# A new order for side work in a two-layer encoder kernel: modulation slots, the last norms of attention, and squares

## The reference

```python
mod = silu(c) @ w_ada[l] + b_ada[l]              # 6 vectors of 1024 per sequence: shift, scale, gate, twice
h = rms_norm(x, g_attn) * (1 + scale_a) + shift_a
q_a, k_a, v_a, c_q, c_kv, k_r = split(h @ w_in)  # group A: 8 heads, 2 kv heads; group B: latent attention, 8 heads
o_a = attention(rope(rms(q_a)), rope(rms(k_a)), v_a)
o_b = attention(q from rms(c_q) @ w_uq, k and v from rms(c_kv) @ w_ukv)
x = x + gate_a * (concat(rms_norm(o_a), rms_norm(o_b)) @ w_o)
h = rms_norm(x, g_ffn) * (1 + scale_f) + shift_f
u = depthwise_conv_3(h @ w_up)                   # 2 x 2816 channels
x = x + gate_f * ((silu(gate) * val) @ w_down)
```

## Time and profile before

| | |
|---|---|
| median of 3 runs | 1179.14 us (1178.0 to 1182.05) |
| profiled execution | 1182.05 us, span 1180.1 us |
| TensorE busy | 1147.2 us, 97% |
| VectorE busy | 747.7 us, 63% |
| GpSimd busy | 580.4 us, 49% |
| ScalarE busy | 507.9 us, 43% |
| DMA | 151.68 MB, mean 129 GB/s |

### The profile page before, as it was taken

The page is one execution under the profiler, slowest core; times in us unless marked ns, Lnnn a source line. Parts: engine busy times, 40 slices in busy tenths (PEclk is TensorE's granted clock), DMA queues, the critical chain, the costliest instruction groups (busy, mean ns, idle before and its releaser), DMA issues.

```text
span 1180.1 us, 18741 instructions
## 1 busy us (share of the span) xinstructions
PE 1147.2 (97%) x6264; PEld 955.4 (81%) x6264; DVE 747.7 (63%) x1466; ACT 507.9 (43%) x922; POOL 580.4 (49%) x783
## 2 busy tenths in 40 slices
PE   9999999999999999998999999999999999999996
PEld 6897677898888887787898966799888888888886
DVE  5888666767767777688666687746774133312445
ACT  5345764354422344133444567535443134423442
POOL 2482342645555355536766324244555445454462
PEclk9999999999999999998999999999999999999998
DMA  9843620424455444554433221022433222332222
GB/s 347 322 159 122 220 73 19 161 72 161 160 174 201 165 143 173 196 179 160 149 119 108 72 72 37 19 72 82 145 131 108 96 85 95 99 107 89 89 89 72
DMA packets 44123, 151.68 MB, mean 129 GB/s; under 512 B 5138, under 2 KB 7954, under 8 KB 44052
## 3 DMA queue, kind: packets, MB, share of 16 engines
q1 hardware_dynamic: 44052, 150.77, 36.8%
HBM read 148.65 MB, written 2.10 MB: 128 GB/s over the span
## 4 chain that ended last, share of the span: by engine, by line
PE 35%; issue 31%; POOL 21%; POOLq 11%; DVE 1%; DVEq 0%; ACT 0%; ACTq 0%
POOL w_lo L600 21%; PE ps L687 11%; PE ps L688 11%; PE ps L693 11%; POOLq L602 7%; POOLq L660 2%; POOLq L658 1%; PE ps L819 1%; PE ps L808 1%; PE ps L788 0%; DVE ada_prod L1716 0%; PE ps L796 0%; DVE x L1655 0%; POOLq L613 0%; DVE h_lo L1759 0%
## 5 line engine op out<-in xcount | busy, mean ns | idle before, releaser
L600 POOL TENSOR_TENSOR w_lo<-w_raw,w_hi 128x256 fp32r<-128x256 f32 x712 | 540.4, 789 | 478.0 <-ACT w_hi L1243 445.6
L687 PE MATMUL ps<-h_hi,w_hi 128*128 128x512 f32 (+1 forms) x864 | 318.0, 368 | 5.7 <-POOLq L603 5.6
L688 PE MATMUL ps<-h_lo,w_hi 128*128 128x512 f32 (+1 forms) x864 | 317.1, 367 | 0.0
L693 PE MATMUL ps<-h_hi,w_lo 128*128 128x512 f32 (+1 forms) x864 | 316.7, 367 | 0.0
L1243 ACT CAST w_hi<-w_raw 128x1024 fp32r<-128x1024 f32 x178 | 183.4, 1048 | 197.4 <-PE ps L687 196.8
L2006 DVE SCALAR_TENSOR_TENSOR u_sb<-ps,par,u_sb 128x510 f32<-128x510 f32 x176 | 131.8, 749 | 110.5 <-ACT u_sb L1448 96.5
L687 PEld LDWEIGHTS ps<-h_hi,w_hi 128*128 128x128 f32 x864 | 163.8, 190 | 33.2 <-POOLq L603 6.8
L693 PEld LDWEIGHTS ps<-h_hi,w_lo 128*128 128x128 f32 x864 | 163.9, 190 | 26.7
L688 PEld LDWEIGHTS ps<-h_lo,w_hi 128*128 128x128 f32 x864 | 163.9, 190 | 26.0
L687 PE MATMUL ps<-a_hi,w_hi 128*128 128x512 f32 (+1 forms) x400 | 147.0, 367 | 4.1 <-DVEq L1703 4.1
L693 PE MATMUL ps<-a_hi,w_lo 128*128 128x512 f32 (+1 forms) x400 | 146.2, 365 | 0.0
(11 more groups left out here) (181 smaller groups left out, 1496.1 us busy)
## 6 DMA issues: line engine op xcount, KB each, us to landing
w_raw<-w_slots SPq DMA_DIRECT2D x178, 512.0 KB, 3.5
ada_raw<-ada_slots SPq DMA_DIRECT2D x88, 512.0 KB, 4.0
shift<-shift_slots SPq DMA_DIRECT2D x8, 512.0 KB, 12.8
x_tok<-x_rows SPq DMA_DIRECT2D x4, 512.0 KB, 9.9
x<-x_t SPq DMA_DIRECT2D x4, 512.0 KB, 13.8
y_t<-x SPq DMA_DIRECT2D x3, 512.0 KB, 2.9
y_t<-x SPq DMA_DIRECT2D x1, 256.0 KB, 2.9
y_t<-x SPq DMA_DIRECT2D x2, 128.0 KB, 2.7
```

Of the source, the lines that this page charges most:

```text
L600: nc.gpsimd.tensor_tensor(w_lo[:, j, c], w_raw[:, j, c], w_hi[:, j, c].bitcast(F32), ALU.subtract)
L687: hh = mm(out, stat[0], mov[0], start=first, stop=False)
L688: hl = mm(out, stat[0], mov[1], start=False, stop=False)
L693: return mm(out, stat[1], mov[0], start=False, stop=last)
```

## The change

It moves work within the queues and removes or adds none.

- In the plan, group 0's up-projection has 11 takes of modulation slots where it had 8, group 1's 12 where it had 11; the last down tile (7) of groups 0 and 1 has one take where it had 4; and layer 1's input projection has two at its first place, where it had none. These are full-length slots. As all later slots keep their order, the loads move with them.
- In attention TensorE does `group_spread(0)` one turn later, after `scores(13)`. VectorE's four `output_scaled` and four `output_lo` and ScalarE's four `output_hi` are spread over the turns in another way.
- In the norm after attention ScalarE squares tile e before it casts the next weight slot.

```diff
-    ups = [[1] * 8, [1, 2, 1, 2, 1, 2, 1, 1], [2, 2, 1, 1, 1, 0]]
-    downs = [[0, 1, 1, 1, 1, 1, 1, 4], [0, 1, 1, 1, 1, 1, 1, 4], [0] * 8]
+    ups = [[2, 1, 2, 1, 2, 1, 1, 1], [2, 2, 1, 2, 1, 2, 1, 1], [2, 2, 1, 1, 1, 0]]
+    downs = [[0, 1, 1, 1, 1, 1, 1, 1], [0, 1, 1, 1, 1, 1, 1, 1], [0] * 8]
...
-    plan += [((1, "in", n), SLOTS + at, takes) for n, at, takes in ((2, S_UQ, 1), (3, S_UQ, 1))]
+    plan += [((1, "in", n), SLOTS + at, takes) for n, at, takes in ((1, 6, 2), (2, S_UQ, 1), (3, S_UQ, 1))]
...
@@ TensorE, turns of attention
                     if i + 1 < NA:
                         fill(i + 1)
+                    if i == NA + 5:
+                        group_spread(0)
...
-                    if i == NA + 4:
-                        group_spread(0)
@@ ScalarE, turns of attention
-                    if NA + 5 <= i <= NP:
-                        output_hi(L, i - NA - 5)
+                    if i in (NP - 2, NP - 1):
+                        output_hi(L, i - NP + 2)
+                    if i == NP:
+                        output_hi(L, 2)
+                        output_hi(L, 3)
@@ ScalarE, norm after attention
                 for e in range(N_UPD - 4):
+                    square(2 * L + 1, e)
                     if e < TAIL:
                         split_hi(L, S_WO + 4 + e)
-                    square(2 * L + 1, e)
@@ VectorE, turns of attention
-                    if NA + 4 <= i < NP:
-                        output_scaled(L, i - NA - 4)
+                    if NA + 5 <= i < NP:
+                        output_scaled(L, i - NA - 5)
                     if i == NP - 1:
+                        output_scaled(L, 3)
                         output_lo(L, 0)
+                    if i == NP:
                         output_lo(L, 1)
-                    if i == NP:
-                        output_lo(L, 2)
-                        output_lo(L, 3)
                 take_outputs(NP - 2)
+                output_lo(L, 2)
+                output_lo(L, 3)
```

## The result

The changed kernel takes 1192.4 us in the median of 7 runs (1189.54 to 1198.38), the kernel before on the same chip 1182.05 us in 7 runs (1178.0 to 1185.48): 10.4 us more. The ratio is 1.0098 with a 95% interval of 1.0068 to 1.0129. So it is slower, as forecast, and inside the range (1177 to 1193), but well above the 1186.5 us named: 5.9 us, of which 2.9 us is the base (the forecast added its sum to the first median, 1179.14 us) and 3.0 us is the sum, +7.4 forecast and +10.4 measured.

What follows compares the result with a forecast made beforehand. TensorE, busy 97% of the span, was taken to bound the kernel. Terms 8.0 + 0 + 1.3 + 5.2 - 0.3 - 6.8 + 0 = +7.4 us on 1179.14 gave 1186.5 us, range 1177 to 1193.

Steps and rivals of the forecast that it cites:

- Part 1, idle times: Tail of attention: TensorE idles 2.2 and 1.9 us for late output_lo; loss taken 4.0 us per layer, 8.0 in two.
- Part 1, the clock: Tail of attention: lower clock behind the idle times, priced at 0 to 3.4 us over two layers, taken as 0.
- both costs of waiting weigh more: Rival: idle times in attention also bring the lower clock, +3.4, 1190 us; chance 0.15.
- Part 2: Norm after attention, layer 0: squares ahead of casts delay GpSimd's split chain, loss 1.3 us, bounds 0 and 2.5; layer 1: 0.
- the bound of 0: Norm after attention: lower bound of the 1.3 us loss, if a lighter overlap makes it up.
- The sign that was named for it: Timeline of the changed kernel: the stall in the output projection longer than 2.39 us.
- Part 3, group 0: Feed-forward group 0: VectorE's extra takes delay down tile 2, loss 3.6 us plus 1.7 of lower clock; 5.2 taken.
- The part that was to come sooner: Up-projection of group 0: the split after tile 1 moves by 2.8 us, with some 1.5 us before its use.
- Group 1: Feed-forward group 1: 2.08 us stall becomes about 1.8, -0.3 taken; bound -3.8 if it goes with its slow clock.
- Group 2: Up-projection of group 2: tile 1 begins at about 529.6, the 3.63 us stall and slow clock go, gain 6.8 us.
- Part 4: Layer 1's input projection: two full-length slots fit in VectorE's 8.62 us wait, cost 0; 1 us if not.
- The faster rival: Feed-forward: all stalls go with the four-take pile-ups, 11 us won; decides if attention costs under 7 us; chance 0.14.

Runs made afterwards that it cites:

- run 7: Kernel before with the attention part alone, but output_lo(1) back in turn 15, only output_lo(2) and (3) late: 1187.80 us, ratio 1.0049.
- run 8: Kernel before with the attention part alone, but output_lo(2) and (3) back in turn 16, only output_lo(1) late: 1189.05 us, ratio 1.0073.
- run 9: Kernel before with group_spread(0), output_scaled and output_hi as changed, all output_lo in their old turns: 1181.02 us, ratio 0.9994.
- run 1: Kernel before with the attention part of the change alone, old plan and old order of squares: 1193.93 us, ratio 1.0110.
- its repeat: Kernel before with the attention part of the change alone, measured once more: 1195.14 us, ratio 1.0108.
- Run 3: Kernel before with only ScalarE's squares put ahead of the casts in the norm after attention: 1182.99 us, ratio 1.0007.
- run 4: Changed kernel with output_lo(1) back in turn 15 and (2), (3) in turn 16: 1177.27 us, ratio 0.9963 to the kernel before.
- run 2: Kernel before with the new plan of modulation takes alone: 1179.49 us, ratio 0.9970.
- run 11: Kernel before with changed group_spread(0), output_scaled, output_hi, old output_lo turns and squares, retuned takes, two in layer 1's input projection: 1172.73 us, ratio 0.9926.
- run 5: Kernel before with the attention part alone plus 28 unread small matmuls in each of the two waits at out_part: 1208.29 us, ratio 1.0222.
- run 6: Kernel before with the attention part alone plus 8 unread small matmuls in each of the two waits at out_part: 1193.22 us, ratio 1.0091.
- run 10: Kernel before with two takes for four in group 1's last down tile and two in layer 1's input projection: 1176.64 us, ratio 0.9955.

## Why the prediction was right, and where it was not

**Part 1, idle times: right.** The two crossing waits are where they were forecast, and runs 7, 8 and 9 show them to be two separate ones. 2.2 and 1.9 us forecast, 1.96 and 1.88 found; `output_lo(1)` forecast from 182.7, for 1.15 us, found at 184.86 - 1.57 (the shift of turn 15) = 183.3, for 1.15. +4.0 a layer forecast, 8.4 / 2 = 4.2 measured. The 0.38 us wait for `output_lo(0)` was not in the sum. On that 1.15 us the Trainium skill ("SBUF — State Buffer", section "SBUF: two separate sides") has the rule that such a VectorE operation and GpSimd take turns for a whole instruction. Here GpSimd's square of 0.61 us and `output_lo` began within 0.02 us of each other, and `output_lo` took 0.47 us more than the 0.68 us of one that ran alone (at 182.34 in the changed kernel), somewhat less than a full turn; the row was the better price.

**Part 1, the clock: the step that failed.** The prediction said: "I price it at 0 to 3.4 us over two layers (one stretch of 1.7 us each) and take 0." The runs show the lower clock in both layers: 3.3 us in the profile of the changed kernel, at the upper bound, and 4.6 us (3.4 and 1.2) in run 1 and its repeat, above it. There, in layer 0, it began in the work between the two idle times and lasted past the second, and not for one stretch of 1.7 us. The value taken, 0, had a row against it, the 2.08 us stall with its 0.57; the reason given for it, short gaps at clock 1.00 in this stage, came from gaps of under 1 us. The rival "both costs of waiting weigh more" (+3.4, 1190 us) had the mechanism, with a chance of 0.15. Part 1 as a whole, +8.0 forecast and +13.0 measured, is the term that was mis-sized.

**Part 2: mechanism right, size too large.** The cast comes late as forecast: GpSimd's first split begins 211.10 - 208.41 = 2.69 us after `update_x` where it was 202.07 - 200.72 = 1.35, 1.34 us later (forecast 1.3). But from there to the product at the second stall it takes 225.32 - 211.10 = 14.22 us, where it was 217.18 - 202.07 = 15.11: the bound of 0 named a lighter overlap that makes it up, and 0.9 of the 1.3 us was made up. Run 3 finds +0.8, not to be told from 0. The sign that was named for it, a stall longer than 2.39 us, did not come: it is 2.07 us, with 0.71 us a slot ahead.

**Part 3, group 0: the loss to the number, its clock not.** VectorE's work from the first taps to `update_x` was forecast at 342.65 - 258.31 = 84.34 us. In VectorE's timeline after the change:

```profile
266.08 3.27 DVE L2010 SCALAR_TENSOR_TENSOR u_sb<-ps,par,u_sb 128x510 f32<-128x510 f32 x4 [6.17 <-ACT u_sb L1451]
...
350.35 1.87 DVE L1704 SCALAR_TENSOR_TENSOR x<-ps,mod,x 128x256 f32<-128x256 f32 x4
```

That is 84.27 us. The loss was 3.5 us (3.6 forecast), the last idle 1.76 (about 2.0). The part that was to come sooner, a split that moves by 2.8 us and has 1.5 us of room, is there too:

```profile
288.94 0.50 PE L687 MATMUL ps<-h_hi,w_hi 128*128 128x512 f32 x1 [1.30 <-POOLq L603]
```

The 1.7 us of lower clock that the forecast added to this group did not come in this profile (1.00 from 352 to 357); it did in the plan alone (0.70 from 347 to 351, after 1.86 us) and not in run 4 (after 1.83 us). **Group 1:** 2.08 became 1.52 us, below the forecast 1.8, and the lower clock behind it went, which the bound of -3.8 held open. **Group 2: right.** The 3.63 us and their clock are gone; tile 1's taps, forecast at 529.6 on the old time axis, begin at

```profile
538.68 3.28 DVE L2010 SCALAR_TENSOR_TENSOR u_sb<-ps,par,u_sb 128x510 f32<-128x510 f32 x4
```

and 538.68 - 10.7 = 528.0 is 8 us earlier than 535.97. Groups 1 and 2 together won 0.6 + 8.3 = 8.9 us, where -0.3 and -6.8 were taken: 1.7 us of that is the lower clock behind 473.05. By this profile the plan is worth 3.5 - 8.9 = -5.4 us; run 2, where the lower clock did follow the stall in group 0, measured -3.5. The forecast had -1.9 (5.2 - 0.3 - 6.8).

**Part 4: right.** Four instructions fill VectorE's idle time in layer 1's input projection, and 1.68 us of the 8.62 is left:

```profile
665.12 0.20 DVE L1833 RECIPROCAL st_lat<-st_lat 128x8 f32<-128x8 f32 x1 [1.68 <-ACT st_lat L1350]
```

**The sum.** +8.0, +1.3, -1.9 was forecast; +13.0, +0.8, -3.5 was measured. An error of +5.0 in part 1, nearly all of it the clock (4.6), was partly hidden by two of -0.5 and -1.6, which is luck. The faster rival's condition, an attention price under 7 us, is what runs 4 and 11 produce, and they land at 1177 and 1173 us.

## What to carry to other kernels

When an instruction is moved later in one engine's queue, look for the pair of queues that cross: here TensorE waits for VectorE with work queued behind the wait that VectorE needs before it can release the next one, and each of the two crossings cost 2.2 us. Price a new idle time of about 2 us with the lower clock behind it as at least an even chance, and don't take 0 for it: in the traces here (14 profiles, from 120 us to the last norm) it came with or within 2 us behind 38 of 65 stalls of 1.5 to 2.4 us and all nine of 3.6 us. Then find out whether something slower sets the pace behind it, for then the clock costs nothing. Spread side work by the room of the stage: three takes more in a group whose VectorE was full cost 3.5 us, while two takes moved away from just ahead of a group won 5.3 us.

## What the runs showed of the hardware beyond that

The same stall does not always bring the lower clock. After 2.08 us in group 1 the granted clock was 0.57 before; in run 9, at the same place and after the same 2.08 us (the product begins at 474.00), it stayed up:

```profile
474.00:478.00 4.00, 4.00 (x18) 1.00 0.96 353
```

The 1.69 us stall at the last norm of layer 0 (611 to 634 us by the kernel) had the lower clock behind it in the changed kernel and in runs 1, 5, 6, 10 and 11 and the repeat of run 1, and not before nor in runs 2, 3, 4, 7, 8 and 9. The Trainium skill ("TensorE: Matmul & The Clock Gate", section "What's actually happening") says that the gate's watch runs free of the kernel, so that the moment of a change differs from run to run. The traces agree: the clock of 0.60 from 182 to 186 us in run 1 puts the fall 0.7 us behind 182.06, where the product behind the first idle time begins, and the 0.66 from 186 to 192 us in its repeat puts it 1.9 us behind 186.04, the start of the same product. How the same stall at another start time comes to differ wasn't tried.

The lower clock cost nothing where GpSimd set the pace. In layer 0's output projection two products 5.03 us apart wait for it; with the clock down in between, as before, the second waits 0.41 us, and with the clock up, as in run 9, 1.90 us, at the same distance. Then the lower clock comes behind the second stall, where nothing hides it: in run 9 the stretch from the first of them to the norm took 239.80 - 216.91 = 22.89 us, where it was 238.83 - 217.18 = 21.65.

The start of the kernel, which the change doesn't touch, varies by up to 4.4 us between the profiled executions (the same modulation product on TensorE early in layer 0's attention begins at 110.5 to 114.9 us): the absolute times of two single profiles are to be compared from there on.
